# Activation buffers 16 bytes further on, and dense products of 512 columns made as two of 256

## What is computed

```python
proj = (n @ w_in[l]).astype(f32)                     # first block: 1024 -> many columns
merged = sigmoid(gate_r) * (y_rwkv @ p_rwkv) + sigmoid(gate_a) * (y_attn @ p_attn)
h = h + merged @ w_out
h = h + memory_cross_attention(...)                  # four more 1024x1024 products
h = h + square(relu(rmsnorm(h) @ ffn_w1)) @ ffn_w2   # 1024 -> 4096 -> 1024
# second block, twice:
x = x + g1 * token_mix(h, w_in, w_fourier, w_ret, w_out)
x = x + g2 * conv_ffn(h, ffn_up, conv_w, conv_b, ffn_down)   # 1024 -> 5632, 2816 -> 1024
```

## Time and profile before

| | |
|---|---|
| median of 3 runs | 2905.43 us (2904.99 to 2905.44) |
| profiled execution: span from first to last instruction | 2902.9 us |
| median less that span | 2.5 us |
| TensorE (matmul) | 2885.3 us busy, 99% |
| TensorE (weight loads) | 2415.3 us, 83% |
| GpSimd, VectorE, ScalarE | 1585.3, 1570.4, 1109.4 us (55%, 54%, 38%) |

### The profile page before, as it was taken

How to read it: one execution, slowest core, us unless ns; L and a number is a source line. 1 busy time by engine, 2 the same in 40 slices (tenths; PEclk the granted TensorE clock), 3 DMA queues, 4 the chain that set the end, 5 groups by cost and what they waited for, 6 DMA issues and landing times.

```text
span 2902.9 us, 49417 instructions
## 1 busy us (share of the span) xinstructions
PE 2885.3 (99%) x19658; PEld 2415.3 (83%) x19658; DVE 1570.4 (54%) x2227; ACT 1109.4 (38%) x1689; POOL 1585.3 (55%) x1912
## 2 busy tenths in 40 slices
PE   9999999999999999999999999999999999999998
PEld 7877777788888888888888898888898888988887
DVE  5467888424556666775434274435763441473635
ACT  4454445333443332443433243333433342342323
POOL 6432233355546666577544556565584444565654
PEclk9999999999999999999999999999999999999999
DMA  4211111233326687433222223232333222232232
GB/s 173 95 46 42 43 55 54 98 138 102 125 85 226 234 280 261 165 124 123 86 87 72 94 88 111 90 106 87 111 126 109 79 89 84 88 102 95 95 102 73
DMA packets 92292, 322.21 MB, mean 111 GB/s; under 512 B 10144, under 2 KB 14368, under 8 KB 91808
## 3 DMA queue, kind: packets, MB, share of 16 engines
q1 hardware_dynamic: 84544, 302.39, 31.6%
q10 hardware_dynamic: 7520, 16.67, 1.7%
HBM read 315.09 MB, written 3.93 MB: 110 GB/s over the span
## 4 chain that ended last, share of the span: by engine, by line
PE 98%; issue 1%; POOL 1%; DVE 1%; DMA 0%; ACT 0%; POOLq 0%; SPq 0%; ACTq 0%; DVEq 0%
PE bank L906 25%; PE bank L910 25%; PE bank L907 25%; PE bank L1254 2%; PE bank L899 2%; PE bank L901 2%; PE bank L900 2%; PE bank L1265 2%; PE bank L1273 1%; PE bank L934 1%; PE bank L936 1%; PE bank L935 1%; PE bank L958 1%; PE bank L960 1%; PE bank L1786 1%
## 5 line engine op out<-in xcount | busy, mean ns | idle before, releaser
L837 POOL TENSOR_TENSOR w_lo<-w_raw,w_hi 128x256 fp32r<-128x256 f32 x1736 | 1420.4, 853 | 984.7 <-ACT w_hi L1863 974.0
L906 PE MATMUL bank<-act,w_hi 128*128 128x512 f32 (+1 forms) x3464 | 1312.1, 379 | 4.2 <-POOL w_lo L837 1.9
L910 PE MATMUL bank<-act,w_lo 128*128 128x512 f32 (+1 forms) x3464 | 1292.0, 373 | 0.0
L907 PE MATMUL bank<-act,w_hi 128*128 128x512 f32 (+1 forms) x3464 | 1290.9, 373 | 0.0
L906 PEld LDWEIGHTS bank<-act,w_hi 128*128 128x128 f32 x3464 | 652.4, 188 | 127.0 <-issue 8.9
L910 PEld LDWEIGHTS bank<-act,w_lo 128*128 128x128 f32 x3464 | 652.2, 188 | 115.5
L907 PEld LDWEIGHTS bank<-act,w_hi 128*128 128x128 f32 x3464 | 652.9, 188 | 106.2
L1863 ACT CAST w_hi<-w_raw 128x1024 fp32r<-128x1024 f32 (+1 forms) x438 | 454.1, 1043 | 338.0 <-DMA w_raw<-in_weights 156.2
L1871 ACT ACTIVATE arena<-bank 128x512 f32<-128x512 f32 (+1 forms) x177 | 104.1, 592 | 416.9 <-PE bank L910 400.3
L855 POOL TENSOR_TENSOR stats<-stats,exponent 128x8 f32<-128x8 f32 (+2 forms) x38 | 46.6, 1226 | 296.6 <-DVE stats L2918 150.2
L2604 DVE TENSOR_TENSOR act<-tmp,act 128x512 fp32r<-128x512 f32 (+1 forms) x140 | 122.2, 873 | 77.2 <-ACT act L1890 72.7
(11 more groups left out here) (362 smaller groups left out, 3067.7 us busy)
## 6 DMA issues: line engine op xcount, KB each, us to landing
w_raw<-in_weights SPq DMA_DIRECT2D x471, 512.0 KB, 3.5
arena<-in_ada SPq DMA_DIRECT2D x96, 512.0 KB, 4.7
arena<-in_strips ACTq DMA_DIRECT2D x8, 448.0 KB, 3.6
arena<-in_x ACTq DMA_DIRECT2D x1, 2048.0 KB, 11.0
y_scratch<-tmp ACTq DMA_DIRECT2D x7, 256.0 KB, 2.0
arena<-y_scratch ACTq DMA_DIRECT2D x1, 1792.0 KB, 7.9
arena<-in_dft ACTq DMA_DIRECT2D x2, 777.5 KB, 4.3
arena<-in_x SPq DMA_DIRECT2D x3, 512.0 KB, 7.3
```

The lines of the kernel that those rows point to most:

```text
L837: ins = nc.gpsimd.tensor_tensor(w_lo[:, k, cols], weights_of(u)[:, cols], w_hi[:, k, cols].bitcast(F32), ALU.subtract)
L906: nc.tensor.matmul(o, wh, xh, start=first, stop=False)
L907: nc.tensor.matmul(o, wh, xl, start=False, stop=False)
L910: mm = nc.tensor.matmul(o, wl, xh, start=False, stop=last)
```

## The change

An unused tensor of 4 words is declared ahead of the activation buffers, and one of 60 words behind them. In `tile`, the columns are cut into parts of at most `W2` = 256, and each of the three products is issued once for each part. The three kinds stay in their order: both parts of high by high, then both of high by low, then both of low by high. Only the first instruction of a tile has `start`. Where `half` is given or `n` is 256 there is one part, as before. The products of `T["rows"]` are not cut.

```diff
+        sb("ahead_of_acts", [P, 4])
         with nc.sbuf_tensor("arena2", [P, 2 * KT * S], F32) as arena2:
             pass
         acts = {"A2": sb("act2", [P, 2, KT, S], F32R), "A1": sb("act1", [P, 2, KT, S], F32R)}
...
         acts["YA"] = sb("act_attn", [P, 2, 2, S], F32R)
+        sb("behind_acts", [P, 60])
...
                 cols = slice(0, n) if half is None else half_cols(half)
+                parts = [slice(c, min(c + W2, cols.stop)) for c in range(cols.start, cols.stop, W2)]
...
-                        xh, xl = src[:, 0, k, cols], src[:, 1, k, cols]
-                        o = dst[:, cols]
-                        nc.tensor.matmul(o, wh, xh, start=first, stop=False)
-                        nc.tensor.matmul(o, wh, xl, start=False, stop=False)
+                        xh, xl = src[:, 0, k], src[:, 1, k]
+                        for part in parts:
+                            nc.tensor.matmul(dst[:, part], wh, xh[:, part], start=first and part == parts[0], stop=False)
+                        for part in parts:
+                            nc.tensor.matmul(dst[:, part], wh, xl[:, part], start=False, stop=False)
                         if inside:
                             inside()
-                        mm = nc.tensor.matmul(o, wl, xh, start=False, stop=last)
+                        for part in parts:
+                            mm = nc.tensor.matmul(dst[:, part], wl, xh[:, part], start=False, stop=last and part == parts[-1])
```

## The result

The changed kernel takes 2959.11 us (median of 4 runs, 2958.61 to 2959.82) against 2905.27 us before (4 runs, 2904.99 to 2905.44): +53.8 us, a ratio of 1.0184 with a 95% interval of 1.0169 to 1.0198. Of all executions in this document one, of e6_whole_48, took twice as long as the rest (5806 us) for a reason that is not known, and it is left out of that run's ratio.

A forecast was written before the change was run, and what follows sets the result against it. TensorE's stream of matmuls was taken to bound the kernel. Terms of +82.8 us for dense products, -3.7 for existing halves and -1 for waits summed to +78 us on a 2902.9 us span, giving 2984 us, range 2955 to 3025.

The forecast's parts named there:

- A half product costs its overhead again: Dense products: some 13 ns beside the columns belongs to each instruction, so two halves at 119.8 ns cost 13.0 ns more.
- The repeated weights save nothing: Dense products: each part loads its weights again although wh repeats, so no saving is set against the cut.
- The shift: Moved activations: halves take 118.0 ns, the pace of the spectrum's products, so 8808 products cost +9.4 ns each, +82.8 us.
- second sign of being wrong: Prediction wrong if a moving operand whole 16-byte lines off behaves unlike both neighbours that bounded it; no size given.
- The bounds from the retention: Whole products with a shifted operand take 231.9 and 234.3 ns in the retention, against 226.6; halves bounded at 127.5 ns.
- The exchanged products: L899 to L901, activations as stationary operand: 672 products at 0 to +7.7 ns, at most +5 us, taken as 0.
- The -1 us for waits: TensorE's waits shrink when it is slower; of the 1.9 us of its costliest wait, -1 us was counted.
- The spectrum: Products from `spectrum`, neither cut nor shifted within 64 bytes beyond the layout's general move, should keep their pace of 118.0 ns.
- Rival 1: Dense products: the shift does nothing and halves stay at 119.8 ns, +114.5 us, 3019 us; chance 0.37.
- Rival 3: Dense products: a second part with the same weights adds only 2.5 ns, +22 us, 2927 us; chance 0.04.
- Rival 4: Dense products: the shift costs per instruction as in the retention, halves up to 127.5 ns, +250 us, 3155 us; chance 0.06.
- Rival 2: Dense products: the shift ends SBUF collisions, halves go towards 106.7 ns (break-even 113.3), -117 us, 2788 us; chance 0.07.

The follow-up runs named there:

- e6_whole_48: Changed kernel with whole 512 column products and activations set by hand 48 bytes past a multiple of 64: 2939.04 us, ratio 1.0116.
- e1_shift_whole: Changed kernel with both unused tensors kept but dense products left whole at 512 columns: 2955.93 us, ratio 1.0175 against the kernel before.
- e2_halves_only: Changed kernel without both unused tensors, so products are cut but buffers not shifted: 3014.22 us, ratio 1.0375 against the kernel before.
- e7_halves_48: Changed kernel's halves with activation views set by hand 12 words into longer buffers, meant as 48 bytes past a multiple of 64: 2932.47 us, ratio 1.0095.
- e12_weights_144: Halves, with w_hi and w_lo moved by 144 bytes and activations by 256, so all activation buffers stand 112 from the weights within 256: 3004.25 us, ratio 1.0341.
- e3_all_shifted: Changed kernel with the 4 unused words ahead of w_hi instead, so weights and activations move by the same 32 bytes: 3014.08 us, ratio 1.0378.
- e9_halves_112: Changed kernel's halves with activation buffers lengthened and set by hand 112 bytes past a multiple of 128: 2946.13 us, ratio 1.0141.
- e4_halves_16: Changed kernel's halves with activation views set by hand 4 words into longer buffers, meant as 16 bytes past a multiple of 64: 2991.72 us, ratio 1.0298.

## Why the prediction was right, and where it was off

**What bounds the kernel.** Right. The chain is 97% PE, the clock didn't move and the waits hardly did, and the runs' times followed the steps of their products.

**A half product costs its overhead again.** Right in mechanism at the placement of before, and only there: in the changed kernel two halves cost what one whole costs (+3.2 us against e1_shift_whole). With the alignment of before, halves take 120.00 ns in long stretches (119.8 was read from short ones), and e2_halves_only has +108.9 us. 8808 x 13.3 = 117.4 is 8 us more. Those come back around the dense stretches: what the dense products take beyond their own step, for the most part where one follows or precedes a product of another kind, sums to 44.6 us in the trace before and 36.5 us in that of e2_halves_only.

**The repeated weights save nothing.** Right: as many loads as matmuls, and equal steps for first and second parts.

**The shift.** Right in sign, mis-sized, and this is the term that made the prediction 25 us too high. It was "8808 products, each from 226.6 to 2 x 118.0 = 236.0 ns: +9.4 ns, +82.8 us". Measured is 2 x 116.67 = 233.3 ns, 8808 x 6.67 = +58.7 us. The row taken for it, the spectrum's, stood elsewhere: 12 bytes past a multiple of 16 with 256 and 258 columns mixed. No row of before had 256 columns at 32 bytes from the weights, and the table shows steps between 113.4 and 120.5 for neighbouring places; nothing before could have told 118.0 from 116.7. The prediction's own second sign of being wrong came true here: with the operand two whole lines of 16 bytes off, 116.7 ns lies below both neighbours, 118.0 and 119.8. That the time fell inside the range is in part luck, since the lower end was halves at 116.4. The bounds from the retention were right for what they were: a whole product at this shift costs 233.3 ns, between 231.9 and 234.3.

**The smaller terms.** The half products made before gained 1632 x 3.33 = 5.4 us (with those of `folded_tile` -3.7 was counted). The exchanged products, taken at 0 with at most +5, cost 480 x 6.67 = +3.2 us; those are the ones of 512 columns, and of the 384 column ones nothing is counted. The -1 us for waits didn't come: the wait counted there rose from 1.9 to 2.7 us, and no other moved by more than 0.4 us; this is in the next term. What the dense products take beyond their own step is 43.9 us against 44.6. Sum: 58.7 - 5.4 + 3.2 - 0.7 = 55.8 us, against 54.2 of span; 1.6 us are left.

**The spectrum.** Said to stay at 118.0, as "neither cut nor shifted within 64 bytes". That was wrong about the layout: everything behind the activations moved by 288 bytes, since both unused tensors are rounded up. From the timeline of PE, 50 products in 5.92 us, 118.4 ns against 118.0:

```profile
1353.33 0.28 PE L963 MATMUL bank<-arena_r,w_hi 128*128 128x258 f32 x1
...
1359.25 0.28 PE L963 MATMUL bank<-arena_r,w_hi 128*128 128x258 f32 x1
```

**The rivals.** Rival 1, that the shift does nothing, is refuted by e1_shift_whole and e2_halves_only. With it goes the rule of the Trainium skill (SBUF — State Buffer, "Door 1: The DMA port swizzle") as it was used: a shift by whole lines of 16 bytes touches as many lines and yet moved the step, down by 3.3 ns for halves and up by 6.7 for whole products. The Trainium skill speaks there of accesses that cross lines and not of where an operand begins, so what failed is the use that was made of it. Rival 3, that parts with the same weights are cheap, is refuted by the equal steps in e2_halves_only. Rival 4, halves as dear as the retention's products, by 116.7. Rival 2, a place that ends the collisions, didn't happen, but was nearer than its "3.6 times the largest that any row shows": at 112 bytes halves took 113.4 ns, the very break-even of 113.3 that the prediction worked out. No kernel had all buffers at 113.4. By estimate from e7_halves_48, some 5,500 products of act2 at 4.9 ns less would give about 2905 us, the time of before. The one kernel with all of them at that distance, e12_weights_144, got 116.7 to 120.0 ns and 3004 us, so no run supports the estimate, and no version that ran beat the kernel before.

## What to carry to other kernels

In a stream of matmuls that each load their own weights, read the step between starts and compare it with the columns over the clock: the rest, 13 ns of 227 here, is paid by each of two halves in full at one placement (288 clocks against 544), and at another two halves cost no more than a whole (280 against 560). So a cut that looks free in one layout costs 3.7% in the other. Two edits to such a stream have to be measured apart as well as together (+50.6 and +108.9 made +53.8). An unused tensor, or a buffer some bytes longer, is an edit to TensorE's pace: log where the moving operand and the weights stand before comparing two versions. And read the step in more than one layer: a table of addresses and steps from a single stretch forecast 2900 us for a kernel that took 3004.

## What the runs showed of the hardware

- The step of a 256 column product ran from 113.4 to 120.5 ns and that of a 512 column one from 226.7 to 233.3, over the placements of activations and weights in SBUF that ran, with the granted clock at 0.998 to 0.999 of full speed (its 2.4 GHz level) in every traced execution. At the common place whole products had 226.7 ns, the least of the table, and halves 120.0, near its most.
- The place of the weights counts for the pace of matmuls: moved together with the activations by 32 bytes they undo the shift (3014.1 against 2959.1 us, 120.0 against 116.7 ns). The Trainium skill (TensorE: Matmul & The Clock Gate, "Step-by-step: what each phase is for") says that loading the next weights doesn't take read bandwidth from the running matmul. That alone would not let one expect these runs: of e3_all_shifted and the changed kernel, which differ in nothing but the place of w_hi and w_lo, the products of the one take 3.3 ns more. Whether the two reads meet, and where, was not shown.
- `act1` and `act2` in one kernel, with the same view offset, differed by 4.9 ns a product in both layers (e7_halves_48); when act1 stood at 240 and act2 at 112 within 256, it was act2 that had the shorter one (e9_halves_112).
- The same products at the same addresses can run at different paces in one execution: 2742 products of e12_weights_144 at 118.4 and 120.0 ns in two layers, and `act1` of e4_halves_16 at 118.3 and 120.0.
